# Splitting every remaining narrow product group in two column halves and adding them in one VectorE pass

## The chip, the cores and the metric

The kernel runs on one NeuronCore of a Trainium2 chip. The metric is the device time of one execution in microseconds (us). TensorE (PE in the rows; PEld is its weight load) multiplies into the accumulators (PSUM). VectorE (DVE), ScalarE (ACT) and GpSimd (POOL) work element by element, and SyncE (SP) issues the weight transfers.

## What is computed

The reference is one block of gated linear attention, dilated attention and an MLP, followed by a two-layer block with four SwiGLU feed-forward nets, a convolution module and latent attention (MLA). There are 256 tokens and the model width is 1024. All of it is float32. Cut to the products that matter here:

```python
h = rmsnorm(x, ln1);  parts = h @ w_in                      # q, k, v, r, attention, gates
mix = (sigmoid(g_gla) * (o @ w_o_gla) + sigmoid(g_att) * (o_att @ w_o_attn)) @ w_out
x = x + mix
x = x + square(relu(rmsnorm(x) @ w_mlp1)) @ w_mlp2
x = rmsnorm(x + sigmoid(rmsnorm(x) @ w_pg) * (p @ w_pp))
for i in range(2):
    h = h + 0.5 * (silu(n(h) @ w1) * (n(h) @ w3)) @ w2      # ffn1
    h = h + (conv_module(n(h)) if i == 0 else mla(n(h)))
    h = h + 0.5 * (silu(n(h) @ w1) * (n(h) @ w3)) @ w2      # ffn2
return n(h)
```

## The kernel before

Every large product runs as a list of phases (`Phase`), each with groups of W = 256 output columns. A group takes its weights in blocks of up to four slices of 128 rows. SP loads a block into a ring of eight slots, ACT rounds it to float32r (L1037, the high part), and DVE subtracts to get the low part (L1320). ACT and DVE do this five and four blocks ahead of the group in hand (`ahead`). Inputs are stored as a high and a low part as well. So one product of 128 rows by 128 columns by 256 tokens, called a pair below (one row slice, one half of the group's columns), is the sum of three terms: high by high, high by low, and low by high.

`Phase.halves` (L150) says for each group which of two forms it takes.

- **Wide** groups use two matmuls for a pair. `high` (L612) streams the high and low parts of the input at once, 512 columns, into the two halves of the accumulator. `low` (L618) adds the third term to the second half with 256 columns. Within a block all `high` stand together and all `low` stand together, except in the last block of a phase's first group, where they alternate pair by pair.
- **Narrow** groups use three matmuls of 256 columns for a pair (L660), all into one half.

Wide before are all groups of the phases in the list `WIDE`, except the last group of those that do not merely keep their result. The accumulators have two banks. A group uses the bank of the group two before it, and its first matmul waits until `val_done` says that this bank is free.

DVE takes a group's result out in `evacuate` (L1357). For a wide group ACT first copies the second half (`take_lohalf`, L1065), DVE adds both into `val` (L1370), which frees the bank, and the operation proper reads `val`. For a narrow group the operation proper reads the accumulator, and DVE's queue frees the bank after it (`taken`, L1365). Orders are fixed by program order on each engine. In DVE's program a group first prepares the blocks ahead, then does norm and attention steps that are due there, then evacuates. For `resid` it then adds squares, adds to x (L1478, L1481), splits the next input (L1335, L1338) and sums squares for the next norm (L1533, L1538), which PE adds over the partitions (L706).

Steps named later: attention heads lie between the groups of `gates` (scores L851, softmax on DVE and ACT, transposes L710, ACT's copies L1163 and L1164, value products L867 and L872, DVE's copy L1642). The phases `y_gla`, `y_att`, `w_pg` and `w_pp` have one group each. `conv` products are L897. MLA runs through `mla_a`, `mla_kr`, `uq_rope`, `uq_nope`, `ukv_nope` and `ukv_v`, with its heads in between. The phase names of the layers are `ffn1_up0`, `ffn1_down0` and so on.

Of the kernel before, what the change touches and what calls it, by code (L numbers as in the profile page):

```python
# [23 lines left out]
ALU = mybir.AluOpType  # L24
AX_X = mybir.AxisListType.X
# [7 lines left out]
W = 256  # L33
# [92 lines left out]
def lin(const, coeff, i):  # L126

    return const if i is None or coeff == 0 else i * coeff + const

class Phase:
# [16 lines left out]
        yield list(range(first + per * turns, self.groups)), None  # L148

    def halves(self, g):  # L150

        return self.name in WIDE and (g < self.groups - 1 or self.evac[0] in ("keep", "keep_tok"))

# [4 lines left out]
def program(nc, a, out):  # L158

    with ExitStack() as ctx:  # L160
        def sb(name, shape, dt=F32):
            return ctx.enter_context(nc.sbuf_tensor(name, shape, dt))

        def sem(name):
            return ctx.enter_context(nc.semaphore(name))
# [14 lines left out]
        val = sb("val", [P, 2, T])  # L180
# [45 lines left out]
        ps = ctx.enter_context(nc.psum_tensor("ps", [P, 2, 2, 512], F32))  # L226
# [3 lines left out]
        def units(u, n=1):  # L230
            return plain[:, u:u + n, :] if u < 64 else extra[:, u - 64:u - 64 + n, :]
# [7 lines left out]
        def bcast(ap, n):  # L239
            return ap.unsqueeze(1).to_broadcast([P, n, ap.shape[-1]])  # L240
# [100 lines left out]
        blocks, nblk, ngrp, ngate, nkept, nlow = [], 0, 0, 0, 0, 0  # L341
        GATES = {"func": 1, "swiglu": 0.5, "glu": 0.5}
        for p in phases:
            p.block0, p.group0, p.gate0, p.kept0, p.low0 = nblk, ngrp, ngate, nkept, nlow
            nlow += sum(p.halves(g) for g in range(p.groups))
            nkept += p.groups if p.evac[0] in ("keep", "keep_tok") else 0
            nblk += p.groups * len(p.kns)
            ngrp += p.groups
            ngate += int(p.groups * GATES.get(p.evac[0], 0))
            blocks += [(p, g, j) for g in range(p.groups) for j in range(len(p.kns))]  # L350
# [118 lines left out]
        val_done = sem("val_done")  # L469
# [543 lines left out]
        def _(act):  # L1013
# [45 lines left out]
            def take_lohalf(p, g, i, per):  # L1059

                G = p.group0 + g
                act.wait_ge(used, lin(p.block(g, len(p.kns) - 1) + 1, RING if i is not None else 0, i))
                if G >= 2:
                    act.wait_ge(val_done, lin(G - 1, per, i))
                nc.scalar.copy(lohalf[:, G % 2, :, :], ps[:, G % 2, :, T:2 * T]).then_inc(lohalf_done, 1)  # L1065

            def square_pair(name, c, src):
                q = pairs[name][0] + c
                if name == "conv":
                    pe_did(act, f"conv{c}")  # L1070
                else:
                    act.wait_ge(new_x, new_x_at[name] + (0 if name in SILENT else c + 1))
                if q >= 2:
                    act.wait_ge(summed, q - 1)
                if name == "ln_f":
                    for k in range(2):
                        last = act_fn(sq[:, q % 2, k, :], src[:, k, :], ACT.Square,
                                      scale=gain_sq[:, 2 * c + k:2 * c + k + 1])
                    last.then_inc(squared, 1)
                else:  # L1080
                    act_fn(sq[:, q % 2, :, :], src, ACT.Square).then_inc(squared, 1)  # L1081
# [8 lines left out]

            def evacuate(p, g, i, per):
                kind = p.evac[0]
                if p.halves(g):
                    take_lohalf(p, g, i, per)
                if kind == "func":
                    n = p.gate0 + g
                    act.wait_ge(gate_in, n + 1)
                    act_fn(units(p.evac[2] + 2 * g, 2), t1[:, :, :], p.evac[1]).then_inc(gate_out, 1)
                if kind in ("swiglu", "glu") and g % 2 == 0:
                    n = p.gate0 + g // 2  # L1100
                    act.wait_ge(gate_in, lin(n + 1, per // 2, i))
                    act_fn(gated[:, :, :], t1[:, :, :], ACT.Silu if kind == "swiglu" else ACT.Sigmoid  # L1102
                           ).then_inc(gate_out, 1)
                if kind in ("resid", "ple"):
                    c = p.evac[1] if kind == "ple" else g
                    if kind == "ple":
                        act.wait_ge(new_x, new_x_at["ln_f"] + c + 1)
                        for k in (2 * c, 2 * c + 1):
                            last = act_fn(parts[:, 22 + k, 0, :], x[:, k, :], ACT.Copy, scale=gain_both[:, k:k + 1])
                        last.then_inc(ple_high, 1)  # L1110
                    square_pair(pair_of[p.name], c, x[:, 2 * c:2 * c + 2, :])
                if kind == "out":
                    for t in range(NT):
                        act.wait_ge(new_tok, 2 * g + t + 1)
                        act_fn(sq[:, g % 2, t, :], x_tok[:, t, g * W:(g + 1) * W], ACT.Square,
                               accum_out=sum_tok[:, t, g:g + 1]).then_inc(squared_tok, 1)
                if kind == "keep_sq":
                    square_pair("cq" if g < 2 else "ckv", g % 2, units(2 * g, 2))
# [86 lines left out]
            for p in phases:  # L1205
                for groups, turns in p.segments():
                    if turns is not None:
                        with act.Fori(0, turns) as i:
                            for g in groups:
                                for j in range(len(p.kns)):  # L1210
                                    ahead(p, g, j, i)
                                evacuate(p, g, i, len(groups))
                        continue
                    for g in groups:
# [6 lines left out]
                        if p.name == "ffn2_up1" and g in (19, 20):  # L1221
                            t = g - 19
# [13 lines left out]
                        if p.evac[0] == "out" and g == 3:  # L1236
                            load_table(ACT.Sqrt)
                        evacuate(p, g, None, 0)
                        if (p.name, g) in GLA_AT:
                            gla_step(GLA_AT[p.name, g])  # L1240
# [52 lines left out]
        def _(v):  # L1293
            vec = nc.vector
# [16 lines left out]
            def keep(p, g, ins):  # L1311

                ins.then_inc(kept, 1)
                v.wait_ge(kept, p.kept0 + g + 1)
# [27 lines left out]
            def after_split():  # L1342

                if halves[0]:
                    v.wait_ge(ready, lin(halves[0], halves[1], loop[0]))
# [11 lines left out]
            def evacuate(p, g, i, per):  # L1357
                kind, nch, G = p.evac[0], p.width // P, p.group0 + g
                r2 = bcast(rstd[:, :], nch)
                total = ps[:, G % 2, 0:nch, 0:T]  # L1360

                def taken():

                    if not p.halves(g):
                        v.sem_inc(val_done, 1)  # L1365

                if p.halves(g):
                    v.wait_ge(lohalf_done, lin(p.low0 + g + 1, per, i))
                    after_split()
                    TT(val[:, :, :], total, lohalf[:, G % 2, :, :], ALU.add).then_inc(val_done, 1)  # L1370
                    v.wait_ge(val_done, lin(G + 1, per, i))
                    total = val[:, :, :]
                else:
                    v.wait_ge(used, lin(p.block(g, len(p.kns) - 1) + 1, RING if i is not None else 0, i))
                    after_split()
                if kind == "keep":
                    r = rstd2 if p.name in ("ukv_nope",) else rstd
                    scale = p.evac[2] if len(p.evac) > 2 else 1.0
                    keep(p, g, STT(units(p.evac[1] + 2 * g, nch), total, scale, bcast(r[:, :], nch),  # L1379
                                   ALU.mult, ALU.mult))  # L1380
                    taken()
                if kind == "keep_sq":
                    name, c = ("cq" if g < 2 else "ckv"), g % 2
# [25 lines left out]
                if kind in ("swiglu", "glu") and g % 2 == 1:  # L1409
                    n, c = p.gate0 + g // 2, lin(g - 1, per, i)  # L1410
# [22 lines left out]
                if kind == "relu2":  # L1433

                    c = lin(2 * g, 2 * per, i)
# [12 lines left out]
                if kind == "mix":  # L1448
# [5 lines left out]
                    c = (8 if n < 2 else 24) + 2 * n  # L1454
# [33 lines left out]
                if kind == "ple":  # L1488
                    c = p.evac[1]
# [237 lines left out]
            for p in phases:  # L1727
                if p.name == "pw1":
                    v.wait_ge(used, p.block0)
                for groups, turns in p.segments():  # L1730
# [16 lines left out]
                    for g in groups:  # L1747
# [42 lines left out]
                        if p.name not in ("w_pg1", "w_pg2", "w_pg3") and p.evac[0] != "ple":  # L1790
                            evacuate(p, g, None, 0)
# [28 lines left out]
                        if (p.name == "gates" and g % 2 == 0 and g) or p.name == "y_gla0":  # L1820
                            h = g // 2 - 1 if g else 3
# [233 lines left out]
```

## Time and profile before

| | us |
|---|---|
| median of 3 runs | 1495.26 (1495.07 to 1495.51) |
| the profiled execution | 1495.37 |
| its span, first to last instruction | 1493.6 |
| PE busy | 1478.4 (99%) |
| DVE busy | 1137.1 (76%) |
| ACT busy | 748.6 (50%) |
| granted TensorE clock, mean | 0.999 |

Times in the rows are microseconds from the span's start unless marked ns. PE's busy time includes the modelled end of each matmul, so the step from one start to the next says more than its length. A bracket at the end of a timeline row is the idle time of that engine before the row and what ended it.

### The profile page before, as it was taken

Reading aid. Unit: us, or ns where it says so; the run is one execution under the profiler, and the core shown is the slowest. Engines: PE = TensorE matmul, PEld = TensorE weight load, DVE = VectorE, ACT = ScalarE, POOL = GpSimd, SP = SyncE. Lnnn points to the kernel's source line nnn. Section 1 sums busy time; section 2 is a strip of 40 time slices with the busy share of each in tenths; the row PEclk is TensorE's granted clock in tenths of the full one; section 3 lists DMA queues with packets and bytes.
Section 4 is the critical chain, followed back from the end, with each engine's and each line's share of the span. In section 5 each row is a group of like instructions: output and inputs, shape, how many; then the busy total and the mean of one; then the engine's idle time right before and its main releaser. Section 6 shows DMA issues by size and latency. Waiting matters only on the chain.

```text
span 1493.6 us, 25200 instructions
## 1 busy us (share of the span) xinstructions
PE 1478.4 (99%) x9769; PEld 1326.4 (89%) x9769; DVE 1137.1 (76%) x1526; ACT 748.6 (50%) x1016; POOL 51.4 (3%) x97
## 2 busy tenths in 40 slices
PE   9999999999999999999999999999999999999997
PEld 7889899998898988888987888898889998888887
DVE  7877766798865788797876877678776698977754
ACT  5645456454443475454545554445544444555443
POOL 4000000200000000000221000000000000000000
PEclk9999999999999999999999999999999999999999
DMA  8646664566656566646632666566665664466553
GB/s 255 177 127 176 190 181 138 166 184 189 192 184 190 162 195 186 189 155 191 212 114 74 188 190 190 157 192 209 190 185 159 198 162 148 140 185 184 165 177 108
DMA packets 267933, 259.73 MB, mean 174 GB/s; under 512 B 15901, under 2 KB 266091, under 8 KB 267840
## 3 DMA queue, kind: packets, MB, share of 16 engines
q1 hardware_dynamic: 265776, 255.36, 57.2%
q0 software_dynamic: 1760, 2.55, 0.7%
q8 instruction: 64, 1.05, 0.3%
q10 hardware_dynamic: 304, 0.53, 0.1%
q14 instruction: 29, 0.24, 0.0%
HBM read 257.34 MB, written 1.07 MB: 173 GB/s over the span
## 4 chain that ended last, share of the span: by engine, by line
PE 61%; DVE 2%; issue 0%; ACT 0%; ACTq 0%; DVEq 0%
PE ps L612 30%; PE ps L618 16%; PE ps L660 12%; PE misc L897 2%; PE misc L842 1%; PE misc L710 0%; PE misc L706 0%; DVE wsplit L1320 0%; PE ps L872 0%; DVE plain L1393 0%; PE ps L897 0%; PE ps L867 0%; DVE plain L1379 0%; PE misc L911 0%; ACT plain L1287 0%
## 5 line engine op out<-in xcount | busy, mean ns | idle before, releaser
L1320 DVE TENSOR_TENSOR wsplit<-raw,wsplit 128x1024 fp32r<-128x1024 f32 (+2 forms) x530 | 583.3, 1131 | 104.2 <-ACT wsplit L1037 93.6
L1037 ACT CAST wsplit<-raw 128x1024 fp32r<-128x1024 f32 (+2 forms) x530 | 494.3, 970 | 175.0 <-DMA raw<-in_ffn_w_dram 86.5
L612 PE MATMUL ps<-xa,wsplit 128*128 128x512 f32 x1552 | 387.9, 392 | 1.0 <-issue 0.9
L612 PEld LDWEIGHTS ps<-xa,wsplit 128*128 128x128 f32 x1552 | 284.7, 188 | 57.9 <-issue 2.4
L612 PE MATMUL ps<-parts,wsplit 128*128 128x512 f32 x1068 | 267.0, 392 | 1.4 <-DVE parts L1349 0.9
L612 PEld LDWEIGHTS ps<-parts,wsplit 128*128 128x128 f32 x1068 | 195.2, 188 | 39.6 <-issue 1.7
L1065 ACT COPY lohalf<-ps 128x512 f32<-128x512 f32 x152 | 89.1, 586 | 281.4 <-PE ps L612 238.0
L618 PE MATMUL ps<-xa,wsplit 128*128 128x256 f32 x1552 | 218.3, 283 | 0.0
L618 PEld LDWEIGHTS ps<-xa,wsplit 128*128 128x128 f32 x1552 | 206.2, 191 | 7.6
L1370 DVE TENSOR_TENSOR val<-ps,lohalf 128x512 f32<-128x512 f32 x152 | 105.1, 691 | 139.3 <-ACT lohalf L1065 138.8
L660 PE MATMUL ps<-xa,wsplit 128*128 128x256 f32 x1368 | 170.0, 284 | 0.4 <-DVEq L1365 0.3
L660 PEld LDWEIGHTS ps<-xa,wsplit 128*128 128x128 f32 x1368 | 166.6, 192 | 2.5 <-DVEq L1365 0.8
L660 PE MATMUL ps<-parts,wsplit 128*128 128x256 f32 x1308 | 160.9, 284 | 0.7 <-DVEq L1365 0.7
L660 PEld LDWEIGHTS ps<-parts,wsplit 128*128 128x128 f32 x1308 | 158.9, 192 | 1.7 <-DVEq L1365 0.9
L618 PE MATMUL ps<-parts,wsplit 128*128 128x256 f32 x1068 | 149.8, 282 | 0.0
L618 PEld LDWEIGHTS ps<-parts,wsplit 128*128 128x128 f32 x1068 | 142.4, 191 | 6.0
L1102 ACT ACTIVATE work<-t 128x512 f32<-128x512 f32 x48 | 30.4, 633 | 103.6 <-DVE t L1406 103.6
L1081 ACT ACTIVATE sq<-x 128x512 f32<-128x512 f32 x32 | 20.0, 631 | 64.4 <-DVE x L1478 41.5
L1349 DVE TENSOR_TENSOR parts<-work,parts 128x512 f32 (+1 forms) x64 | 44.3, 693 | 8.6 <-DVE parts L1348 2.7
L612 PE MATMUL ps<-wsplit,xa 128*128 128x512 f32 x160 | 43.7, 396 | 0.0
L612 PEld LDWEIGHTS ps<-wsplit,xa 128*128 128x128 f32 x160 | 29.3, 188 | 6.6 <-issue 0.9
L1348 DVE CAST parts<-work 128x512 f32 (+1 forms) x64 | 27.4, 429 | 7.5 <-DVE work L1430 5.6
(310 smaller groups left out, 1004.9 us busy)
## 6 DMA issues: line engine op xcount, KB each, us to landing
raw<-in_ffn_w_dram SPq DMA_DIRECT2D x176, 512.0 KB, 3.8
raw<-in_w_in_dram SPq DMA_DIRECT2D x76, 512.0 KB, 3.6
raw<-in_ffn_w_dram SPq DMA_DIRECT2D x96, 384.0 KB, 3.1
raw<-in_w_mlp_dram SPq DMA_DIRECT2D x64, 512.0 KB, 3.7
raw<-in_conv_w_pw_dram SPq DMA_DIRECT2D x24, 512.0 KB, 3.4
raw<-in_ffn_w_dram SPq DMA_DIRECT2D x32, 256.0 KB, 3.1
raw<-in_w_o_gla_dram SPq DMA_DIRECT2D x8, 512.0 KB, 3.6
raw<-in_w_out_dram SPq DMA_DIRECT2D x8, 512.0 KB, 3.8
```

Source lines behind the costliest of these rows:

```text
L612: return mm(ps[:, bank, c, :], still, both.rearrange("p h t -> p (h t)"), start=p.k0[j] + kk == 0, stop=end, skip_group_check=True)
L618: return mm(ps[:, bank, c, T:2 * T], still, moves, start=False, stop=end, skip_group_check=True)
L660: last = mm(ps[:, bank, c, 0:T], still, moves, start=st and n == 0, stop=en and n == 2, skip_group_check=True)
L897: last = mm(conv_out(i, c)[32 * q:32 * q + 32, :], conv_w(2 * i + c)[:, m, q, :], shifted(i)[:, c, q, 4 * m:4 * m + T], start=(m == 0), st ...
L1037: nc.scalar.copy(wsplit[:, slot, 0:kn, 0, 0:p.width], raw[:, slot, 0:kn, 1, 0:p.width]).then_inc(hi_done, 1)
L1065: nc.scalar.copy(lohalf[:, G % 2, :, :], ps[:, G % 2, :, T:2 * T]).then_inc(lohalf_done, 1)
L1081: act_fn(sq[:, q % 2, :, :], src, ACT.Square).then_inc(squared, 1)
L1102: act_fn(gated[:, :, :], t1[:, :, :], ACT.Silu if kind == "swiglu" else ACT.Sigmoid).then_inc(gate_out, 1)
L1320: TT(wsplit[:, slot, 0:kn, 1, 0:p.width], raw[:, slot, 0:kn, 1, 0:p.width], wsplit[:, slot, 0:kn, 0, 0:p.width].bitcast(F32), ALU.subtract ...
L1348: step(vec.tensor_copy(dst[:, :, 0, :], src))
L1349: TT(dst[:, :, 1, :], src, dst[:, :, 0, :].bitcast(F32), ALU.subtract).then_inc(ready, n)
L1370: TT(val[:, :, :], total, lohalf[:, G % 2, :, :], ALU.add).then_inc(val_done, 1)
```

## The change

`halves` is now true for every group of 256 columns. The old condition becomes `by_act` and says only who adds the halves. Where it holds, ACT copies the second half and DVE adds, as before. For all other groups one DVE `tensor_reduce` reads both halves from the accumulator, the two values to be added as the innermost axis (256 elements apart), writes their sum to `val`, and raises `val_done`. DVE waits for that and the operation proper then reads `val`. `taken` no longer does anything in these groups. In `relu2` the last group now takes the one-instruction form (L1437) instead of L1439 and L1441.

Sixty-three groups change: the 8 of `gates`, 4 `y_gla`, 4 `y_att`, 4 `w_pg`, 4 `w_pp`, 8 of `pw1`, 3 of `mla_a`, 2 of `uq_rope`, 4 each of `uq_nope`, `ukv_nope` and `ukv_v`, and the last group of `hr`, `w_out`, `mlp1`, `mlp2`, `pw2`, `w_o`, the four `up` and the four `down` phases. `mla_kr`, of 128 columns, stays narrow.

```diff
     def halves(self, g):
+
+        return self.width == W
+
+    def by_act(self, g):
 
         return self.name in WIDE and (g < self.groups - 1 or self.evac[0] in ("keep", "keep_tok"))
@@
-            nlow += sum(p.halves(g) for g in range(p.groups))
+            nlow += sum(p.by_act(g) for g in range(p.groups))
@@ ACT, evacuate
-                if p.halves(g):
+                if p.by_act(g):
                     take_lohalf(p, g, i, per)
@@ DVE, evacuate
-                if p.halves(g):
+                if p.by_act(g):
                     v.wait_ge(lohalf_done, lin(p.low0 + g + 1, per, i))
                     after_split()
                     TT(val[:, :, :], total, lohalf[:, G % 2, :, :], ALU.add).then_inc(val_done, 1)
@@
                 else:
                     v.wait_ge(used, lin(p.block(g, len(p.kns) - 1) + 1, RING if i is not None else 0, i))
                     after_split()
+                    if p.halves(g):
+                        vec.tensor_reduce(val[:, :, :], ps[:, G % 2, :, :].rearrange("p c (h t) -> p c t h", h=2), AX_X,
+                                          ALU.add).then_inc(val_done, 1)
+                        v.wait_ge(val_done, lin(G + 1, per, i))
+                        total = val[:, :, :]
```

## Rows read from the trace of the kernel before

**Rows 1.** Page, part 1: busy us, share, instructions.

```profile
PE 1478.4 (99%) x9769; PEld 1326.4 (89%) x9769; DVE 1137.1 (76%) x1526; ACT 748.6 (50%) x1016; POOL 51.4 (3%) x97
```

**Rows 2.** Chain that ended last, in order of time: start, us, what.

```profile
647.97 3.65 PE ps L612 x16
651.62 1.91 PE ps L618 x16
655.38 5.75 PE ps L660 x48
```

**Rows 3.** Timeline, first group of `ffn1_up1`: start, us, engine, line, form.

```profile
1015.64 0.40 PE L612 MATMUL ps<-xa,wsplit 128*128 128x512 f32 x1
1015.99 0.40 PE L612 MATMUL ps<-xa,wsplit 128*128 128x512 f32 x1
```

**Rows 4.** Groups of instructions by form: busy us, mean ns of one.

```profile
L1320 DVE TENSOR_TENSOR wsplit<-raw,wsplit 128x1024 fp32r<-128x1024 f32 x388 | 465.5, 1227 | 65.2 <-ACT wsplit L1037 56.0 <-DVE t L1400 1.5 <-DVE t L1406 0.6
...
L1629 DVE TENSOR_REDUCE stat<-logit 128x1 f32<-128x768 f32 x4 | 3.8, 954 | 0.1
```

**Rows 5.** Timeline, DVE: evacuation through `val`, then one from the accumulator.

```profile
203.55 0.69 DVE L1370 TENSOR_TENSOR val<-ps,lohalf 128x512 f32<-128x512 f32 x1 [1.83 <-ACT lohalf L1065]
204.28 0.62 DVE L1393 TENSOR_SCALAR plain<-val,rstd_tok 128x256 f32<-128x256 f32 x2
...
1253.32 0.88 DVE L1393 TENSOR_SCALAR plain<-ps,rstd_tok 128x256 f32<-128x256 f32 x2
1254.35 1.23 DVE L1320 TENSOR_TENSOR wsplit<-raw,wsplit 128x1024 fp32r<-128x1024 f32 x1 [0.16 <-DVE plain L1393]
```

**Rows 6.** Stages: stretch, its us, busy PE, PEld, DVE, ACT, POOL, granted clock, DMA.

```profile
1198.00:1262.00 64.00, 63.10 (x485) 58.69 (x484) 58.82 (x102) 28.93 (x50) 0.00 (x0) 1.00 0.59 170
513.00:543.00 30.00, 29.07 (x224) 27.66 (x222) 27.77 (x41) 22.28 (x36) 0.00 (x0) 1.00 0.68 202
```

**Rows 7.** Timeline, attention heads 0 and 1: ACT's copy, PE's value product.

```profile
222.20 0.80 ACT L1164 COPY work<-misc 128x768 f32<-128x768 f32 x1
223.06 0.71 PE L867 MATMUL misc<-work,plain 128*128 128x128 f32 x4
...
238.16 0.80 ACT L1164 COPY work<-misc 128x768 f32<-128x768 f32 x1
239.63 0.61 PE L867 MATMUL misc<-work,plain 128*128 128x128 f32 x4
```

**Rows 8.** Groups by form, `y` phases: busy us, mean ns, idle before, releaser.

```profile
L1446 DVE TENSOR_TENSOR plain<-ps,plain 128x512 f32<-128x512 f32 x4 | 2.8, 692 | 2.5 <-PE ps L660 2.5
...
L1451 DVE TENSOR_TENSOR work<-ps,plain 128x512 f32<-128x512 f32 x4 | 2.8, 690 | 2.4 <-PE ps L660 2.4
```

**Rows 9.** Timeline, `y` phases into `w_out`.

```profile
306.64 0.69 DVE L1349 TENSOR_TENSOR parts<-work,parts 128x512 fp32r<-128x512 f32 x1
307.57 0.40 PE L612 MATMUL ps<-parts,wsplit 128*128 128x512 f32 x1
```

**Rows 10.** Timeline, into `mlp1`: DVE's last split, PE's use of it.

```profile
328.88 0.88 DVE L1338 SCALAR_TENSOR_TENSOR xa<-x,gain,xa 128x256 fp32r<-128x256 f32 x2
330.09 0.40 PE L612 MATMUL ps<-xa,wsplit 128*128 128x512 f32 x1
```

**Rows 11.** Timeline, `w_pg` and `w_pp`.

```profile
542.65 0.70 PE L706 MATMUL misc<-acc,ones 128*128 128x256 f32 x2 [0.51 <-DVE acc L1538]
```

**Rows 12.** Timeline, MLA.

```profile
1233.19 0.69 DVE L1379 SCALAR_TENSOR_TENSOR plain<-ps,rstd 128x512 f32<-128x512 f32 x1 [0.60 <-PE ps L660]
...
1241.46 4.60 PE L660 MATMUL ps<-parts,wsplit 128*128 128x256 f32 x36 [0.71 <-DVEq L1365]
```

**Rows 13.** Timeline, `pw1`: before the first convolution products.

```profile
744.43 3.96 DVE L1320 TENSOR_TENSOR wsplit<-raw,wsplit 128x1024 fp32r<-128x1024 f32 x2
746.41 7.12 PE L897 MATMUL misc<-plain 128*32 128x256 f32 x128
```

**Rows 14.** Timeline, the last group of all.

```profile
1485.45 0.88 DVE L1462 SCALAR_TENSOR_TENSOR plain<-ps,half_tok,plain 128x256 f32<-128x256 f32 x2 [9.80 <-PE ps L660]
```

## Prediction

> **What bounds the kernel now.** I read the page first: PE is busy 99% of the span and DVE 76% [rows 1]. A busy PE need not be at its pitch, so next I read the chain of waits for the step from one matmul to the next. Sixteen `low` take 1.91 us, sixteen `high` 3.65 us, and 48 narrow matmuls 5.75 us [rows 2]. Nearly all product groups run at this pitch: PE, not the weights, sets the time. Last I looked at DVE stage by stage, because a mean of 76% hides stages with no room. In the MLA stage, from 1198 to 1262 us, DVE is busy 58.8 of 64 us, and in the `w_pg`/`w_pp` stretch 27.8 of 30 us [rows 6]. There PE and DVE are both nearly full. The change takes work from PE and gives work to DVE, so these two stages decide.
>
> **What PE gains.** A group of 16 pairs takes 5.75 us narrow and 1.91 + 3.65 = 5.56 us wide [rows 2]: 0.0125 us a pair. Where `high` and `low` alternate, two pairs start 0.35 us apart [rows 3], against 3 x 0.12 = 0.36 us narrow [rows 2], and I take 0.005 us. The 63 groups hold 944 pairs (2832 narrow matmuls). In the first groups of phases 160 of them fall into the alternating block. The gain is 784 x 0.0125 + 160 x 0.005 = 10.6 us, if all of it counted.
>
> The same number of columns streams either way, so the rows price the matmul that goes away at 12 ns. The Trainium skill (TensorE: Matmul & The Clock Gate, "Wait — 56ns, not 53.3ns?") gives a matmul a fixed cost of 2.5 ns beyond its columns. By it the gain would be an estimated 944 x 2.5 ns = 2.4 us. The rows decide.
>
> **What one pass costs DVE.** The pass reads 1024 elements of a partition and writes 512. Nothing in this trace adds pairs that lie 256 elements apart. The nearest rows: a `tensor_reduce` over 768 contiguous elements takes 0.954 us, and a DVE operation on 1024 elements 1.227 us [rows 4]. I take 1.23 us. Were it to scale straight, 954/768 x 1024 gives 1.27 us. A gain is excluded, since no work of DVE goes. The wait for its own result costs 0.04 us: the operation after L1370 starts 0.73 us later for 0.69 us of work. Against that, an operation that reads `val` no longer releases the bank through the queue: from the accumulator the queue's step leaves 0.16 us idle before the next one, from `val` 0.03 to 0.04 us [rows 5]. That returns 0.13 us. Net: 1.23 + 0.04 - 0.13 = **1.14 us** for each group on DVE. On the way to ACT, which starts at the operation's end, nothing returns: 1.27 us.
>
> The other end of this cost: if elements so far apart came at half rate, the pass would take 1.23 + 1024 x 1.05 ns = 2.3 us (1.05 ns being what each element adds between the two rows, (1227 - 954)/256). I take the low end, because it is nearest in kind.
>
> The bank itself is freed by the pass, before the operation proper: 1.23 us after the group's end in place of 0.69 + 0.13, so 0.4 us later. Groups of 5.6 us on PE hide that.
>
> **Where the passes lie, stage by stage.**
>
> *Last groups of long phases* (`hr`, `mlp1`, the four `up`): the next phase needs their result only late in its first group, and DVE has room. Cost nothing. If that cover were gone it would be 1.1 us each.
>
> *`gates` and attention heads.* An odd group's pass sits between a head's normalisation and ACT's sigmoid, and ACT's copies of the probabilities stand behind that sigmoid. At head 0 the copies end at 223.00 us and PE's value products start at 223.06: no room. At head 1 they end at 238.96, and PE comes at 239.63: 0.67 us [rows 7]. I take that for heads 2 and 3 too. The path grows by 1.27 us a head, and at head 0 I add half of the pass of group 0, 0.6 us, as it stands before the softmax. So 1.9 + 3 x 0.6 = 3.7 us, and PE's gain here is lost in waiting.
>
> *`y` phases.* From `y_gla1` on seven passes add 7 x 1.14 = 8.0 us to DVE. It waited 2.5 + 2.4 us for PE before these evacuations, a quarter of the 2.5 at `y_gla0` [rows 8], so 4.3 us are absorbed. `w_out` needs the last part at 307.57 us, 0.24 us after it is ready [rows 9]. That leaves 8.0 - 4.3 - 0.2 = 3.5 us. Together with the heads **7.2 us**.
>
> *Into the next phase after a `resid` group.* The pass lengthens the way to the split of x, whose first piece is ready at 328.88 + 0.44 = 329.32 us, with PE's use at 330.09: 0.8 us of room [rows 10]. An added 1.14 us and an earlier PE leave 0.5 us. There are six like it besides the one into `pw1` (after `w_out`, `mlp2`, `pw2`, `ffn2_down0`, `ffn1_down1`, `w_o`): **3.0 us**.
>
> *`w_pg` and `w_pp`.* From the norm at 513 us DVE goes from one operation to the next, and at 542.65 us PE waits for the sum of squares that stands behind all of it [rows 11]. Eight passes: **9.1 us**. The queue is in program order, so the blocks ahead stand behind the passes too, and there is nothing to overtake them.
>
> *`pw1`.* Two passes stand before the copies that the first convolution needs. These end where the next blocks begin, at 744.43 us, for a start at 746.41 [rows 13]: 2 us of room against 2.3 us, 0.5 us into the phase, and PE earlier by 0.7. Later groups wait for PE anyway, and PE keeps its gain there. With the last copies I take a net **0.4 us**.
>
> *MLA.* Seventeen passes, 19.4 us. The four of `ukv_v` return 0.26 us each, since the two operations behind it read `val` (0.62 us for 0.88 [rows 5]): 1.0 us. One wait of 0.6 us for PE is absorbed, and PE already waits 0.71 us for DVE's bank [rows 12]. The rest of the 5.2 us idle [rows 6] are gaps between dependent operations, which stay. **17.8 us.**
>
> *The end.* DVE sits idle for 9.8 us before the last evacuation [rows 14], so its pass lies open: **1.2 us**.
>
> **The sum.** Costs: 7.2 + 3.0 + 9.1 + 0.4 + 17.8 + 1.2 = 38.7 us. The gain that remains is that of the last groups, whose PE is the bound: 384 pairs x 0.0125 = 4.8 us. Net +33.9 us on the profiled execution's 1495.37 us (its span is 1493.6) gives 1529.3. The median of the runs shown is 0.1 us lower: **1529 us**, 2.3% slower.
>
> **The rivals.**
>
> *The passes are hidden (faster).* DVE prepares weights four blocks ahead, and this lead could take up the passes. Then PE's 10.6 us count, less the 4.2 us of boundaries and end: 1489 us. It would need 18 us of idle DVE in MLA, and there are 5.2 [rows 6]. Against it too: the lead covers weights only, and the results that PE waits for stand in the same queue. 0.06.
>
> *Half hidden.* If half of the passes of MLA and of `w_pg` found gaps, 13.5 us fall away: 1516 us. For it speaks that my walk through these stages adds up every dependence. 0.10.
>
> *A slow pass.* At 2.3 us, some 47 passes on the path cost 1.07 us more each: 1579 us. The pass crosses 256 elements at every step, which no timed row does at length. 0.18. The Trainium skill (Advanced Engine Details and Errata, "PSUM Cachelines") says that the accumulators work in lines of two float32 values and that patterns that do not run on slow matmuls clearly. It says nothing of DVE, and no run here shows it yet.
>
> *Wide saves nothing in these groups.* The change would then not do what it says on PE: 1529 + 4.8 = 1534 us. Against it stand equal steps in every wide group of the chain [rows 2]. 0.05.
>
> *The clock.* PE now waits up to 3 us at a time in MLA and `w_pg`. If its granted clock, 1.00 in both stages [rows 6], fell, narrow stretches would run longer: some 10 us at half speed, 1539 us. 0.06.
>
> **How the numbers follow.** The forecast has 0.55, with 1518 to 1542 as its own range: 36 of the passes lie on the path, and 0.2 us in the pass or 5 us in a stage move it that far. The range from 1512 to 1580 takes in the forecast, nearly all of the half hidden case, the two small ones and half of the slow pass. About 0.2% is what a measurement of this kernel can tell from no change. Faster 0.06, same 0.02, slower 0.92.
>
> **What would show it.** A row for the pass of 128x512 out of 128x1024, 63 times, near 1.23 us. L660 left with the 24 matmuls of `mla_kr`. PE's busy share lower in MLA, which grows from 64 to about 82 us with DVE over 95% busy. PE waits on the pass at bank releases in `ukv_nope`. `w_pg` to the first group of `ffn1_up0` some 9 us longer. If instead MLA keeps its length, the stage was not DVE's, and the whole sum falls. If the pass takes over 1.5 us, its size was wrong and the places right.

## The result and the profile after

The changed kernel takes 1539.4 us against 1495.2 us: 1.029 times the time before, 95% interval 1.028 to 1.031. The forecast was 1529, with a range from 1512 to 1580: the direction and the places held, and the size was 10.4 us too small. The profiled execution took 1539.8 us with a span of 1538.1 us, so the traces differ by 44.5 us.

The page first: busy time, and the clock line of the span in 40 slices.

```profile
PE 1486.2 (97%) x8825; PEld 1286.1 (84%) x8825; DVE 1211.1 (79%) x1588; ACT 748.8 (49%) x1016; POOL 51.7 (3%) x97
...
PEclk9999999999999999999999999999999997999999
```

Against [rows 1], 944 matmuls are gone and DVE is busy 74 us more, but PE's busy time rose by 8 us. Less work and more busy time together point to matmuls that became slower, and the 7 near the end of the clock line says where to look.

The groups of instructions by form: the pass, and what is left of the narrow form (busy us, mean ns | idle before, releaser).

```profile
L1381 DVE TENSOR_REDUCE val<-ps 128x512 f32<-128x1024 f32 x63 | 76.9, 1220 | 21.9 <-PE ps L616 19.2 <-PE ps L622 1.8
...
L664 PE MATMUL ps<-xa,wsplit 128*128 128x256 f32 x24 | 3.2, 290 | 0.0
```

Sixty-three passes of 1.22 us, where 1.23 us was taken from [rows 4]. The narrow form is left only in `mla_kr`. The chain of waits at the end of `ffn1_up0`, where the last group was narrow before [rows 2]:

```profile
670.48 1.91 PE ps L622 x16
672.39 3.65 PE ps L616 x16
676.05 1.91 PE ps L622 x16
677.96 2.07 PE ps L616 x9
```

The last group runs at the steps of the groups ahead of it. PE's gain is real where PE is the bound.

The waits of PE, longest sum first (us in total, times, longest), of the whole execution:

```profile
PE ps L616 <- DVE val L1381: 11.7, 6, 3.1
PE misc L871 <- ACT work L1168: 5.2, 4, 2.0
PE ps L871 <- DVE plain L1402: 4.2, 1, 4.2
PE ps L616 <- DVE parts L1353: 4.2, 2, 3.2
PE ps L616 <- DVE xa L1342: 3.0, 7, 0.5
PE misc L710 <- DVE acc L1533: 2.5, 1, 2.5
```

The first line is what the change brought: PE waits for accumulators that only the pass sets free (before, it waited 1.1 us in all for a bank). The second is the four attention heads, where ACT's copies now come late.

MLA as one stretch (us; busy PE, PEld, DVE, ACT, POOL; granted clock), from the first product of `mla_a` to the first behind the stage:

```profile
1218.40:1315.80 97.40, 82.57 (x427) 66.36 (x426) 87.36 (x148) 34.06 (x70) 0.00 (x0) 0.89 0.39 112
...
1218.40:1298.80 80.40, 66.13 (x345) 54.16 (x343) 77.80 (x114) 28.25 (x46) 0.00 (x0) 0.93 0.48 136
```

Before, the same stretch was 74.5 us with DVE busy 66.4 (the fence under mla_pass_alone). DVE has 21.0 us more work and the stage is 22.9 us longer. Up to the attention DVE is busy 97%.

To see where the time went, I put the start of each phase's first matmul in both traces side by side. The table gives what each stretch grew by in us. The forecast column regroups the terms on record. The last column is the experiment fill_two, below, in which the clock falls in one place only.

| stretch | forecast | change | fill_two |
|---|---|---|---|
| start to `gates` | -0.2 | -0.5 | -0.6 |
| `gates`, heads and `y` | +7.2 | +5.1 | +5.1 |
| `w_out` | -0.2 | +4.8 | +3.4 |
| `mlp1`, `mlp2` | -0.5 | -0.2 | -0.2 |
| `w_pg`, `w_pp`, `ffn1_up0` | +9.4 | +9.4 | +9.4 |
| `ffn1_down0` | -0.5 | -0.5 | -0.5 |
| `pw1` | +0.4 | +2.5 | +2.5 |
| `pw2` to `ffn1_down1` | -0.7 | -0.1 | -0.2 |
| MLA | +18.3 | +22.9 | +18.7 |
| `w_o` to the end | +0.8 | +1.1 | +1.1 |
| sum | +33.9 | +44.5 | +38.8 |

### The profile page after: what moved, and what is told of

The parts are those of the page before. It is cut to its first block, busy times and chain, and to the rows that moved or that the text cites. A ratio compares the mean times of both kernels' runs of the same rounds, so it can differ in the third digit from the quotient of the medians.

```text
span 1538.1 us, 23373 instructions
## 1 busy us (share of the span) xinstructions
PE 1486.2 (97%) x8825; PEld 1286.1 (84%) x8825; DVE 1211.1 (79%) x1588; ACT 748.8 (49%) x1016; POOL 51.7 (3%) x97
## 4 chain that ended last, share of the span: by engine, by line
PE 76%; DVE 17%; issue 4%; ACT 3%; DVEq 0%; ACTq 0%; POOL 0%; POOLq 0%
PE ps L616 47%; PE ps L622 24%; DVE val L1381 4%; DVE wsplit L1324 2%; ACT wsplit L1041 1%; DVE plain L1435 1%; PE misc L714 1%; PE misc L846 1%; DVE plain L1388 1%; DVE rstd L1358 0%; DVE acc L1542 0%; DVE t L1409 0%; DVE val L1374 0%; PE misc L876 0%; ACT L1102 0%
## 5 line engine op out<-in xcount | busy, mean ns | idle before, releaser
L616 PE MATMUL ps<-xa,wsplit 128*128 128x512 f32 x2000 | 507.4, 394 | 7.8 <-DVE val L1381 4.2
L616 PEld LDWEIGHTS ps<-xa,wsplit 128*128 128x128 f32 x2000 | 368.4, 189 | 84.8 <-DVE xa L1342 5.2
L616 PE MATMUL ps<-parts,wsplit 128*128 128x512 f32 x1504 | 390.8, 397 | 12.5 <-DVE val L1381 6.1
L616 PEld LDWEIGHTS ps<-parts,wsplit 128*128 128x128 f32 x1504 | 278.1, 190 | 69.9 <-DVE val L1381 8.2
L622 PE MATMUL ps<-xa,wsplit 128*128 128x256 f32 x2000 | 286.3, 283 | 0.0
L622 PEld LDWEIGHTS ps<-xa,wsplit 128*128 128x128 f32 x2000 | 268.1, 191 | 10.0
L622 PE MATMUL ps<-parts,wsplit 128*128 128x256 f32 x1504 | 224.7, 284 | 0.0
L622 PEld LDWEIGHTS ps<-parts,wsplit 128*128 128x128 f32 x1504 | 207.8, 192 | 8.8
L1381 DVE TENSOR_REDUCE val<-ps 128x512 f32<-128x1024 f32 x63 | 76.9, 1220 | 21.9 <-PE ps L616 19.2
L1106 ACT ACTIVATE work<-t 128x512 f32<-128x512 f32 x48 | 30.4, 632 | 105.7 <-DVE t L1415 105.7
L1085 ACT ACTIVATE sq<-x 128x512 f32<-128x512 f32 x32 | 20.0, 631 | 72.6 <-DVE x L1487 45.9
L616 PE MATMUL ps<-wsplit,parts 128*128 128x512 f32 x192 | 48.8, 394 | 1.4 <-DVE val L1381 1.4
L616 PEld LDWEIGHTS ps<-wsplit,parts 128*128 128x128 f32 x192 | 34.8, 188 | 8.4 <-DVE val L1381 1.6
L1415 DVE TENSOR_TENSOR t<-val,rstd 128x512 f32<-128x512 f32 x48 | 33.2, 692 | 3.3
```

Of the source, the lines that this page charges most:

```text
L616: return mm(ps[:, bank, c, :], still, both.rearrange("p h t -> p (h t)"), start=p.k0[j] + kk == 0, stop=end, skip_group_check=True)
L622: return mm(ps[:, bank, c, T:2 * T], still, moves, start=False, stop=end, skip_group_check=True)
L1381: vec.tensor_reduce(val[:, :, :], ps[:, G % 2, :, :].rearrange("p c (h t) -> p c t h", h=2), AX_X, ALU.add).then_inc(val_done, 1)
L1415: TT(t1[:, :, :], total, r2, ALU.mult).then_inc(gate_in, 1)
```

## The experiments

My theory: passes on a DVE without room make the loss, stretch by stretch, and a clock that falls in PE's new waits makes the rest. The rivals: the loss comes from the wide products and their bank releases; or the way of each result, not DVE's load; or one stretch pays for another.

The clock, by stretch (columns as above), in the change. Each window holds one place where it fell.

```profile
310.00:322.00 12.00, 8.78 (x47) 7.58 (x46) 10.32 (x15) 1.85 (x3) 0.00 (x0) 0.86 0.36 115
540.00:550.00 10.00, 7.23 (x33) 5.91 (x32) 9.67 (x13) 5.38 (x10) 0.00 (x0) 0.83 0.41 111
1240.00:1250.00 10.00, 7.53 (x36) 6.42 (x35) 9.72 (x14) 4.47 (x7) 0.00 (x0) 0.83 0.19 53
1268.00:1282.00 14.00, 10.91 (x47) 8.68 (x46) 13.63 (x17) 4.00 (x4) 0.00 (x0) 0.76 0.45 132
1296.00:1312.00 16.00, 12.64 (x55) 9.17 (x55) 9.27 (x27) 4.39 (x19) 0.00 (x0) 0.68 0.00 1
```

**fill: all five waits filled.** Five edits of one kind (in `ukv_nope` ahead of two groups); two of them:

```diff
+            def busy_products(out, n):
+                for _ in range(n):
+                    mm(out, ones[:, :], cos[:, :], start=True, stop=True, skip_group_check=True)
@@ input_there, first group of w_out, k = 6
+                            dv_did(pe, "att3.o")
+                            busy_products(misc[:, 3, 0:T], 6)
@@ mla_head, step pv, h = 0
+                        pe.wait_ge(val_done, by["w_o"].group0 - 1)
+                        busy_products(ps[:, by["w_o"].group0 % 2, 0, 0:T], 8)
```

> The full change, and in five of PE's waits products whose result is not used (6 in w_out, 5 ahead of w_pg3, 4 ahead of the ckv sum, 3 and 6 in ukv_nope, 8 ahead of the first value product, each about 0.46 us, in all less than the waits themselves), so that PE does not stand idle there. DVE's work is the same. Theory (the granted clock of 0.5 in five stretches of together 29 us costs PE about 10 us beyond the passes): 1529 us, between 1527 and 1533, granted clock 1.00. Rival (in these stretches DVE sets the time and the clock only follows): within 2 us of 1539.

Measured: 1535.5 us (1534.8 to 1535.8), granted clock 0.999. Neither number came: 3.9 us came back of the 10. By the starts of phases, `w_out` gained 1.35 us and the way from `ukv_v` to `w_o` 4.15 us; what was gained at `w_pg3` (1.55 us) was lost again by `ffn1_up0`, and the fill at the `ckv` sum left nothing either. So the clock explains about half of what the forecast lacks, and only in two places.

**fill_two: only the two waits shown above.**

> The full change with products of unused result in only two of the five waits: 6 in w_out and 8 ahead of the first value product of MLA's attention. The run with all five gave 1535.5 us against 1539.4, and against the trace of the full change it gained 1.35 us in w_out and 4.15 us on the way from ukv_v to w_o; the falls of the clock at w_pg3, at the ckv sum and in ukv_nope (14 us at 0.5 together) gained nothing that lasted, since DVE sets the time there. Theory (a low clock costs only where PE's products, not DVE, are the bound): these two give all of it, 1535.5 us, between 1534.5 and 1536.5, with the clock still falling in the three other places. Rival (each stretch at 0.5 costs by its length): 1537.5 to 1538 us.

Measured: 1534.5 us (1534.2 to 1535.0), 1.0 us less than with five, which lies within the intervals of the two ratios (1.025 to 1.028, and 1.025 to 1.029). The same stretches as above, in fill_two:

```profile
310.00:322.00 12.00, 11.38 (x66) 9.81 (x65) 11.59 (x17) 3.11 (x4) 0.00 (x0) 1.00 0.39 115
540.00:550.00 10.00, 7.52 (x42) 6.35 (x42) 9.66 (x13) 5.21 (x8) 0.00 (x0) 1.00 0.57 158
1240.00:1250.00 10.00, 7.41 (x39) 6.33 (x40) 9.72 (x13) 5.85 (x9) 0.00 (x0) 1.00 0.25 72
1268.00:1282.00 14.00, 10.84 (x44) 8.68 (x45) 13.63 (x17) 3.38 (x3) 0.00 (x0) 0.76 0.48 150
1296.00:1312.00 16.00, 16.00 (x100) 12.06 (x99) 12.67 (x43) 7.27 (x30) 0.00 (x0) 1.00 0.00 1
```

I had expected the clock to fall in three other places still; it fell only in `ukv_nope`, the fourth line. That makes the reading stronger: at `w_pg3` the clock stayed up, and still `ffn1_up0` began no earlier against `w_out`'s end (1.5 us before the change's trace at both). In `ukv_nope` it fell, and MLA is 18.7 us longer than before; in fill, where it did not fall, 18.6. In these five places a low clock cost where PE was the bound and nothing that lasted where DVE was. Its price in this change is 1539.44 - 1534.49 = 4.95 us, 5.0 below (5.7 us between the two traces of the table). Whether filling a wait in vain costs something is not shown.

**mla_only: MLA's 17 groups alone.** `halves` returns `self.by_act(g) or self.name in (the five MLA phases)`.

> Only the 17 narrow groups of the MLA stage become wide; all others stay as before. In the trace of the full change the way from the start of mla_a to the start of w_o grew by 22.9 us (199.4 to 222.3 us would be wrong to read here: it is 74.5 to 97.4 us). Theory (DVE is the bound of this stage, and its passes stand on the path): the same 22.9 us come alone, 1518 us, between 1516 and 1520. Rival (part of it is delay carried in from the stages ahead, whose DVE was behind): 1508 to 1513 us.

Measured: 1516.4 us (1514.7 to 1516.6), +21.3. The stage makes its loss by itself; the rival falls. The clock fell there too (0.995 over the span).

**all_but_mla: the rest alone.** `halves` returns `self.width == W` outside these five phases.

> The full change without the MLA stage, which stays narrow. Theory: stages add up, so 1539.4 - 22.9 = 1516.5 us, between 1515 and 1518; the granted clock falls only in the two waits near 315 and 544 us. Rival (stages are coupled, MLA would fill in for what the others lose): 1520 us or more.

Measured: 1519.8 us, +24.6, and 3.3 us over what I expected. Two things make 2.4 of it: I had subtracted the boundary into MLA (1.1 us by the phase starts) with the stage, though it stays, and in this trace the clock fell behind the wait of 2.0 us at the first head too (0.66 from 225 to 230 us), which took 1.3 us. Together the two parts give 45.9 for 44.2 us: they add up, with little coupling.

**mla_pass_alone: the pass without the wide products.** PE's products are those of before.

```diff
+                    if p.name in ("mla_a", "uq_rope", "uq_nope", "ukv_nope", "ukv_v"):
+                        step(vec.tensor_reduce(val[:, :, :], ps[:, G % 2, :, :].rearrange("p c (h t) -> p c t h", h=2), AX_X,
+                                               ALU.add))
```

> PE's products of all groups as before; in the MLA stage alone each of the 17 groups gets the pass of the change as additional work of DVE, its result unused (val is written and not read, the operation behind it still reads the accumulators). Theory (DVE's time alone, not PE's order or its waits, makes the loss): 17 x 1.26 us = 21.4 us less the 0.6 us of a wait that absorbs, about 1516 us; up to 1520 with a fall of the clock. Rival (the loss comes with the wide products, through bank releases and their order): under 1505 us.

Measured: 1519.1 us, +23.9. MLA as one stretch, before, and then in this run:

```profile
1197.90:1272.40 74.50, 73.60 (x557) 66.45 (x555) 66.38 (x129) 34.01 (x70) 0.00 (x0) 1.00 0.51 146
```

```profile
1198.70:1297.40 98.70, 84.42 (x558) 75.12 (x557) 87.57 (x147) 34.04 (x70) 0.00 (x0) 0.88 0.38 112
```

DVE's 21.2 us of passes lengthen the stage by 24.2 us (23.9 by the phase starts) with PE's products as they were; the clock is 0.88. The added passes are the cause in MLA. The wide products are not, and their gain (128 pairs, 1.6 us) does not show there. One thing this run does not separate: the pass also stands ahead of the bank's release here, so the way to the release is longer as well as DVE's load larger. For the load speaks that DVE is busy 97% up to the attention in the change.

**pg_only: the eight groups of `w_pg` and `w_pp` alone.**

> Only the eight groups of w_pg and w_pp become wide. In the full change this stretch grew by 8.7 us (7.2 to the start of ffn1_up0 and 1.5 in its first group). Theory (its own passes on a DVE without room): 1495.2 + 8.7 = 1504 us, between 1503 and 1505, and the clock falls near 535 us. Rival (part of it is delay of DVE that was carried in): under 1501 us.

Measured: 1504.3 us, +9.1, as the sum had it. The clock did not fall near 535 us, though the wait ahead of `w_pg3` was 2.76 us as in the change (2.77): the loss is the passes' and not the clock's.

**heads_y_only: `gates` and the eight `y` groups alone.**

> Only gates and the eight y groups become wide. In the full change the start of w_out came 5.1 us later by these, and w_out itself lost another 4.8 us to parts that were late, of which 1.35 us were the clock. Theory (w_out's loss is DVE's delay of the y groups, paid later): 5.1 + 4.8 = 9.9 us less the boundary, 1504.5 us, between 1503 and 1506, and PE waits 3 us in the middle of w_out's first group. Rival (w_out's loss comes from its own last group): 1500.5 us, and no such wait.

Measured: 1506.2 us, +11.0: the loss in `w_out` is there (5.2 us by the phase starts), and so is the wait inside its first group:

```profile
PE ps L616 <- DVE parts L1353: 3.2, 1, 3.2
```

So `w_out` pays what the `y` phases leave undone on DVE. The measured time is 1.7 us above the number expected. I had subtracted the boundary into `mlp1` there, which by the phase starts is not part of `w_out`'s loss; `w_out` lost 0.4 us more than in the change, and the way from `ukv_v` to `w_o` 0.4.

**pw1_only: `pw1` alone.**

> Only pw1's eight groups become wide. In the full change pw1 grew by 2.5 us. Theory (its own passes ahead of the copies for the first and the last convolution, which have no room): 1497.5 us, between 1497 and 1498. Rival (the pass of ffn1_down0's last group ahead of it makes more than half of it): 1495.5 to 1496.5 us.

Measured: 1496.7 us, +1.5 (interval 0.1 to 3.0), between the two. By the phase starts `pw1` loses 1.3 us with its own passes alone, 0.5 with the pass ahead of them alone (last_only, below), and 2.5 with both: what is left, some 0.7 us, comes only when they meet. Both waits are in the change's trace, at the first convolution products and at the last (start, us, [idle before]):

```profile
766.18 7.11 PE L901 MATMUL misc<-plain 128*32 128x256 f32 x128 [1.57 <-issue]
...
811.47 3.66 PE L901 MATMUL misc<-plain 128*32 128x256 f32 x64 [1.35 <-DVE plain L1435]
```

**all_by_act: wide everywhere, added without the pass.** `by_act` returns `self.width == W`.

> The 63 groups are wide as in the change, but their halves are added as in the other groups: ACT copies the low half (0.59 us of ACT), DVE adds it (0.69 us in place of the pass of 1.22 us). PE's work is that of the change, DVE has 63 x 0.53 = 33 us less. Theory (DVE's time in MLA and w_pg/w_pp makes the loss): the passes there cost 0.69 + 0.04 - 0.13 = 0.60 us in place of 1.13, so about half of the loss goes: 8.7 -> 4.6 us in w_pg/w_pp, 18.6 -> about 9 us in MLA, and the clock falls less: 1510 to 1520 us. Rival (the way of each result, not DVE's load, makes the loss; copy and add together take 1.28 us and more): 1535 us or more. Second rival (ACT waits for each group's end ahead of its copies of weights, and PE then waits for weights): over 1525 us, with waits of PE on ACT.

Measured: 1523.6 us, +28.4: better than the change by 15.9 us, and 3.6 us above the range expected. By the phase starts (of an execution 2.3 us above the median), the way from `gates` to `w_out` now costs nothing (1.0 us is gained where the change lost 5.1), `w_out` loses 1.6, `pw1` 0.6, MLA 15.6 where about 9 was expected. But `w_pg` to `ffn1_up0` loses 14.7 us, more than with the pass. The reason is in the timeline of DVE and ACT there (start, us, [idle before <-releaser]):

```profile
520.84 0.58 ACT L1069 COPY lohalf<-ps 128x512 f32<-128x512 f32 x1
...
521.45 0.69 DVE L1374 TENSOR_TENSOR val<-ps,lohalf 128x512 f32<-128x512 f32 x1 [1.38 <-ACT lohalf L1069]
...
522.18 0.69 DVE L1409 TENSOR_TENSOR t<-val,rstd 128x512 f32<-128x512 f32 x1
...
522.90 0.63 ACT L1102 ACTIVATE plain<-t 128x512 f32<-128x512 f32 x1 [1.48 <-DVE t L1409]
...
529.72 0.58 ACT L1069 COPY lohalf<-ps 128x512 f32<-128x512 f32 x1
...
530.33 0.69 DVE L1374 TENSOR_TENSOR val<-ps,lohalf 128x512 f32<-128x512 f32 x1 [2.47 <-ACT lohalf L1069]
...
531.78 0.69 DVE L1503 TENSOR_TENSOR x<-x,work 128x512 f32<-128x512 f32 x1
...
532.50 0.91 ACT L1113 ACTIVATE parts<-x,gain_both 128x256 fp32r<-128x256 f32 x2 [2.21 <-DVE x L1503]
```

DVE waits for ACT's copy, then ACT waits for DVE's result, group after group: both have time (from 505 to 545 us DVE is busy 30.4 of 40 us, ACT 21.6), and neither uses it. My theory priced load alone; here the rival of the way of each result holds, in this stretch. The second rival falls: PE waits for ACT's copies of weights once, 1.9 us. The clock is not out of it, though. It was 0.83 from 536 to 546 us and 0.76 from 553 to 560, 3.4 us at 0.5 each, for which PE can have paid 3.4 us at the most, so the stretch loses more than with the pass even without them. In MLA it was 0.83 from 1262 to 1272 and 0.63 from 1283 to 1297 us, and how much of the 15.6 us is the clock, how much the load and how much the way, no run separates.

**last_only: the last groups of the phases that were wide already, with the pass.** `halves` returns `self.name in WIDE`.

> Only the last groups of the phases that were wide already become wide (hr, w_out, mlp1, mlp2, pw2, w_o, the eight of the feed-forwards), with the pass; gates, y, w_pg/w_pp, pw1 and MLA stay narrow. By the steps of the full change: PE gives back 0.2 us in hr, mlp1 and each up, 0.5 in each down, 0.8 in mlp2; each resid group costs some 0.7 us at the next phase and the end 1.2: in sum 1496.5 us, between 1495 and 1498. Rival (the boundaries were only late because DVE was behind from other passes): PE's 4.8 us nearly all stay, 1492 us.

Measured: 1498.2 us, +3.0, interval 1.001 to 1.003, just above the range. PE's gains are there (0.5 us in each `down`, 0.8 in `mlp2`, 0.2 in each `up`), and boundaries and MLA take back more. The way from the start of `mla_a` to that of `uq_rope` alone grew by 1.6 us, where I had put 0.7 for that boundary.

**ups_only: only the last groups of `hr`, `mlp1` and the four `up`, with the pass.** `halves` adds these six names.

> Only the last groups of hr, mlp1 and the four up phases become wide. Theory: 6 x 16 pairs x 0.0125 us = 1.2 us less, 1494.0 us, since the pass behind them lies where DVE has room. Rival (each pass pushes back the split that the next phase waits for at its end): no change, 1495.2 us, or up to 1497.

Measured: 1495.1 us, ratio 0.9999, interval 0.999 to 1.001. The six gains of 0.17 to 0.19 us are in the trace (of an execution 0.6 us above the median), and 0.9 us go again at `uq_rope`, 0.4 in `w_pg`/`w_pp` and 0.3 in `w_out`. Ahead of `mla_a` DVE came late after a wait for ACT's copy of weights:

```profile
1195.63 1.23 DVE L1324 TENSOR_TENSOR wsplit<-raw,wsplit 128x1024 fp32r<-128x1024 f32 x1 [3.17 <-ACT wsplit L1041]
```

Before, the longest such wait in this place was 1.8 us. Why the copies came late in this arrangement I have not settled, and that this wait makes the loss at `uq_rope` is not shown.

**gates_ups_act: `gates` and these six, added by ACT's copy.**

```diff
-        return self.name in WIDE and (g < self.groups - 1 or self.evac[0] in ("keep", "keep_tok"))
+        return (self.name in WIDE and (g < self.groups - 1 or self.evac[0] in ("keep", "keep_tok"))) or self.name in (
+            "gates", "hr", "mlp1", "ffn1_up0", "ffn1_up1", "ffn2_up0", "ffn2_up1")
```

with `halves` returning `self.by_act(g)`.

> The version that the runs point to: only gates and the last groups of hr, mlp1 and the four up phases become wide, and their halves are added with ACT's copy and an addition of 0.69 us, not by the pass; the rest is as before. In the run with ACT's copy everywhere these phases lost nothing at their ends: 8 x 0.2 us in gates less what the heads take back (0.3 us were left), 0.2 us in each of the six others. Theory: 1.2 to 1.5 us less than before, 1493.8 us. Rival (as in the run with the passes in the last groups of the ups: MLA, where DVE sets the time, gives it back): 1495 us.

Measured: 1493.3 us (1493.1 to 1493.7), 0.9988 of before, interval 0.998 to 0.9997: 1.9 us faster than the kernel before, and the best of all versions. Its copy and addition (busy us, mean ns):

```profile
L1374 DVE TENSOR_TENSOR val<-ps,lohalf 128x512 f32<-128x512 f32 x166 | 114.8, 691 | 153.3 <-ACT lohalf L1069 152.4
...
L1069 ACT COPY lohalf<-ps 128x512 f32<-128x512 f32 x166 | 97.2, 586 | 288.6 <-PE ps L616 242.9 <-PE ps L622 45.4
```

Fourteen groups more than before take the 0.69 us form, and the trace has no wait of PE for them. By the phase starts 1.4 us are gained in `gates` and the six last groups, as forecast, and 0.2 go again in MLA. But 0.6 us of the difference lie behind the last operation of ACT, where nothing was edited: from its end to the end of the span it is 3.1 us here and in all_by_act, and 3.7 to 3.8 us in every other run and before. Why is open, so not all of the 1.9 us belongs to the products.

## Why the prediction was right, and where it was short

**The pass: right.** 1.22 us for 1.23. A slow pass at 2.3 us, which had 0.18, falls with that row; elements 256 apart cost no more than neighbours. The Trainium skill (Advanced Engine Details and Errata, "PSUM Cachelines") tells of slow matmuls for such patterns; for this DVE pass the trace shows no such cost.

**PE's gain: right where it was counted.** A `down` begins its successor 0.52 us earlier for 44 pairs, 0.0118 us a pair for 0.0125. The estimate by the Trainium skill's 2.5 ns a matmul (TensorE: Matmul & The Clock Gate, "Wait — 56ns, not 53.3ns?") would have been 0.11 us. That the change saves nothing on PE falls with the 0.52 us.

**`w_pg` and `w_pp`: right,** 9.4 us as forecast, 9.1 alone. **The end: right,** -0.5 us of PE and +1.2 us of the open pass give the measured +0.6.

**MLA: right in its cause and, at full clock, in its size** (18.7 for 18.3 with its boundary). DVE is busy 97% up to the attention, PE waits at `ukv_nope` for the pass, and DVE's added work alone gives such a loss (23.9 us at a clock of 0.88, for 22.9 at 0.89). Half hidden and hidden both fall here.

**The clock: in the wrong place of the reckoning.** I had put it as a rival of its own, with 0.06 and 10 us, though it needs the very waits that my forecast makes. It belonged in the sum: the waits of the forecast are its condition. It took 5.0 us. That the time landed on the 1539 us of that rival is half chance, since the other half has other causes. The 10 us were too much too, and in part in the wrong stretches: I named MLA and `w_pg`, and let PE's clock count where DVE was the bound. It cost in `w_out` and at MLA's attention, and nothing that lasted at `w_pg3`.

**Terms that were mis-sized, 4.9 us without the clock.** The heads, the `y` phases and `w_out` together cost 8.5 us at full clock for 7.0. The heads held on PE (the first `y` group begins 4.0 us later by them for 3.7). DVE's way through the `y` phases, before and then in the change (start, us):

```profile
277.49 2.36 DVE L1320 TENSOR_TENSOR wsplit<-raw,wsplit 128x1024 fp32r<-128x1024 f32 x2
```

```profile
271.10 1.23 DVE L1381 TENSOR_REDUCE val<-ps 128x512 f32<-128x1024 f32 x1
...
277.18 1.22 DVE L1381 TENSOR_REDUCE val<-ps 128x512 f32<-128x1024 f32 x1
...
282.22 2.35 DVE L1324 TENSOR_TENSOR wsplit<-raw,wsplit 128x1024 fp32r<-128x1024 f32 x2
...
314.95 0.69 DVE L1353 TENSOR_TENSOR parts<-work,parts 128x512 fp32r<-128x512 f32 x1
```

From the blocks ahead of `y_gla1`'s evacuation (277.49 and 282.22 us) to the last part for `w_out` (306.64 [rows 9] and 314.95 us) DVE's delay grows from 4.7 to 8.3 us: 3.6 us, where the sum had 8.0 - 4.3 = 3.7 for its seven passes. What it left out stands just ahead of them, the passes of the last `gates` group (271.10) and of `y_gla0` (277.18). Counted from the start of `gates`, which comes 0.5 us earlier in the change, DVE is 5.2 us late at `y_gla1`; the sum let it be as late as PE, 3.7. That is the missing 1.5 us, and PE pays most of the delay where the prediction looked for it, at the last part, for which it waits 3.2 us in the middle of `w_out`'s first group.

`pw1` cost 2.5 us for 0.4. I put two passes, 2.3 us, against the room of 2 us [rows 13]; but the pass of the group ahead stands before the copies for the first convolution too, and against the start of `pw1` these end 3.5 us later. I also let later groups go free. The last copies had 0.8 us of room (they ended at 785.70 + 4.31 us, and PE came at 790.85), and against the start of the convolution ahead of them they end 2.3 us later:

```profile
785.70 4.31 DVE L1426 COPY plain<-plain 32x512 f32<-32x512 f32 x7
```

```profile
807.06 4.30 DVE L1435 COPY plain<-plain 32x512 f32<-32x512 f32 x7
```

The boundaries from `mlp1` on measure about 0.8 us where I had 0.5, which makes some 1.1 us in all.

**A count that does not fit.** The forecast's own range rests on 36 passes on the path and the price of the slow pass on some 47. The stretches of the sum hold 45: 4 at the heads, 7 in `y`, 6 boundaries, 8 in `w_pg`/`w_pp`, 2 in `pw1`, 17 in MLA and 1 at the end. The time of the forecast does not hang on it.

## What to carry to other kernels

Moving work off the bounding engine pays only in the stretches where the receiving engine has room, so read both engines stage by stage, and then once more behind the stage, where a queue's delay is paid. A wait that a forecast makes is itself a cause: ask what the waiting engine does next and whether it is the bound then; if it is, a lower clock belongs in the sum, and where another engine is the bound it does not. Where a result goes back and forth between two engines, shifting load to the idle one can be worse than leaving it: count hand-overs as well as microseconds.

## What the runs showed of the hardware that was not expected

The clock did not follow from the length of the wait alone: ahead of `w_pg3` PE waited 2.77 us in the change and in fill_two, and 2.76 in pg_only; the clock fell to 0.5 in the first and stayed at 1.00 in the two others. In all_but_mla it fell behind a wait of 2.0 us at the first head, where it held in the change behind the same wait. It also differs between executions of one kernel: in one of the four of pg_only the mean clock was 0.996 where the others have 0.999, and the time was 1.2 us longer. Fourteen products (12 rows in `w_out`, 16 ahead of the attention, some 0.22 us apart), whose results nobody reads, were worth 5.0 us.

A strided sum of two halves of the accumulators, 1024 elements in, takes 1.220 us, within 1% of a plain operation of 1024 elements in this kernel (1.227 us [rows 4]).
